# Token mixer of a two-layer block: groups of score products and of transposes split around halves of projections

## The reference, cut to what matters

```python
for i in range(DEPTH):                       # DEPTH = 2, 256 tokens, D = 1024
    h = rmsnorm(x, norm_mix[i])
    x = x + token_mixer(h, w_in[i], ...)     # the part that is changed
    x = x + peer(rmsnorm(x, norm_ffn[i]), ...)
return rmsnorm(x, norm_final)

def token_mixer(h, ...):                     # c = h @ w_in, split by columns
    o_ret = retention(q, k, v, g, norm)      # scores * decay, values, norm, gate
    o_moba = moba(q, k, v)                   # causal softmax attention, 4 heads
    o_ssm = mamba2(z, xbc, dt, ...)          # convolution, scores * exp(segment sums), norm
    o_nsa = nsa(q, cmp, slc, win, gate, ...) # compressed, selected and window attention
    return concatenate([o_ret, o_moba, o_ssm, o_nsa]) @ w_out
```

## Time and profile before

| what | value |
| --- | --- |
| runs | 1931.24, 1931.28, 1932.91 us; median 1931.28 |
| profiled execution | 1932.08 us |
| its span, first to last instruction | 1930.2 us |
| granted TensorE clock | 0.997 |
| PE busy | 1909.7 us, 99% of the span |
| DVE, POOL, ACT busy | 1289.6, 1245.1, 996.0 us |
| mixer of layer 0 | about 60 to 166 us of the span |
| mixer of layer 1 | about 1015 to 1122 us |

### The profile page before, as it was taken

The page is one execution under the profiler, slowest core; times in us unless marked ns, Lnnn a source line. Parts: engine busy times, 40 slices in busy tenths (PEclk is TensorE's granted clock), DMA queues, the critical chain, the costliest instruction groups (busy, mean ns, idle before and its releaser), DMA issues. The chain is left out here.

```text
span 1930.2 us, 38013 instructions
## 1 busy us (share of the span) xinstructions
PE 1909.7 (99%) x12350; PEld 1699.9 (88%) x12350; DVE 1289.6 (67%) x2922; ACT 996.0 (52%) x1581; POOL 1245.1 (65%) x626
## 2 busy tenths in 40 slices
PE   9999999999999999999999999999999999999998
PEld 9888888899999888888898888888999998888886
DVE  5656799789997444444466558996899964444444
ACT  5655444654444554455466544447544454455444
POOL 6447788877776555555574477888777765555553
PEclk9999999999999999999999999999999999999999
DMA  6525555554444566555545255555444455555553
GB/s 221 185 89 164 191 191 185 185 173 154 152 160 165 196 189 193 195 194 189 185 164 179 88 175 197 185 187 185 162 161 154 159 170 193 195 191 193 194 196 130
DMA packets 93240, 338.40 MB, mean 175 GB/s; under 512 B 10352, under 2 KB 10736, under 8 KB 93168
## 3 DMA queue, kind: packets, MB, share of 16 engines
q1 hardware_dynamic: 93168, 337.54, 52.0%
HBM read 336.45 MB, written 1.05 MB: 175 GB/s over the span
## 5 line engine op out<-in xcount | busy, mean ns | idle before, releaser
L491 POOL TENSOR_TENSOR WL<-ring,WH 128x1024 fp32r<-128x1024 f32 x360 | 867.7, 2413 | 342.6 <-ACT WH L1405 174.6
L1405 ACT CAST WH<-ring 128x1024 fp32r<-128x1024 f32 x512 | 538.4, 1052 | 695.5 <-PE PS L1099 329.4
L520 POOL TENSOR_TENSOR HX<-G,HX 128x256 fp32r<-128x256 f32 x256 | 371.4, 1451 | 320.9 <-ACT HX L1514 320.9
L2140 DVE TENSOR_TENSOR WL<-ring,WH 128x1024 fp32r<-128x1024 f32 x248 | 303.9, 1225 | 370.9 <-ACT WH L1405 370.9
L1099 PE MATMUL PS<-WH,HX 128*128 128x512 f32 x2048 | 506.2, 389 | 0.0
L1099 PEld LDWEIGHTS PS<-WH,HX 128*128 128x128 f32 x2048 | 384.3, 188 | 79.8
L989 PE MATMUL PS<-HX,WH 128*128 128x512 f32 x1248 | 313.2, 393 | 0.0
L1099 PE MATMUL PS<-WL,HX 128*128 128x512 f32 x1024 | 274.0, 389 | 0.0
L989 PEld LDWEIGHTS PS<-HX,WH 128*128 128x128 f32 x1248 | 224.5, 189 | 40.3
L1031 PE MATMUL PS<-HX,WH 128*128 128x256 f32 x1024 | 255.9, 288 | 0.0
L1032 PE MATMUL PS<-HX,WH 128*128 128x256 f32 x1024 | 250.6, 283 | 0.0
(11 more groups left out here) (262 smaller groups left out, 2084.3 us busy)
## 6 DMA issues: line engine op xcount, KB each, us to landing
ring<-stream SPq DMA_DIRECT2D x636, 512.0 KB, 3.3
X<-x_t SPq DMA_DIRECT2D x4, 256.0 KB, 4.1
out_t<-X SPq DMA_DIRECT2D x2, 512.0 KB, 2.7
CN<-consts SPq DMA_DIRECT2D x1, 851.0 KB, 9.4
WF<-last SPq DMA_DIRECT2D x1, 512.0 KB, 9.7
PR<-params SPq DMA_DIRECT2D x2, 239.0 KB, 4.4
CN<-consts SPq DMA_DIRECT2D x1, 64.0 KB, 3.2
```

What stands on the lines that cost most here:

```text
L491: nc.gpsimd.tensor_tensor(WL[:, b, :], ring[:, slot, :], WH[:, b, :].bitcast(F32), ALU.subtract).then_inc(done, 1)
L520: nc.gpsimd.tensor_tensor(GL[:, s, :], G[:, tile, :], GH[:, s, :].bitcast(F32), ALU.subtract).then_inc(L.gl_ready, 1)
L1405: nc.scalar.copy(WH[:, b, :], ring[:, slot, :]).then_inc(L.hi_ready, 1)
L2140: V.tensor_tensor(WL[:, s % 2, :], ring[:, (U0 + s) % SLOTS, :], WH[:, s % 2, :].bitcast(F32), ALU.subtract).then_inc(L.vlo_ready, 1)
```

## The change

It moves instructions and adds none. (1) The turns of the window branch go in two pairs of heads around unit 13's second half; those of the selected branch around `compress(6)` and unit 14's second half, which now comes before the state-space values. `compress(7)` and the turns of MoBA's queries and keys follow those values at once. (2) MoBA's and the retention's scores go two and two around units 15's and 17's second halves. (3) MoBA's last three turns of probabilities alternate with the retention's values, MoBA's own values wait for the fourth head's copy only before the fourth head, and the fourth `m_turn` comes four halves of the output projection later, behind the first half of piece 2. (4) On ACT the copies and casts follow that order, and the second square root moves behind the third `taken_m`. (5) On DVE `lower_m(0)` goes behind the square of the retention's output, and the second norm's sums behind `lower_m(1)`.

```diff
-                    def turn_group(buf, g):
-                        for h in range(NH):
+                    def turn_group(buf, g, heads=range(NH)):
+                        for h in heads:
...
                     compress(4)
-                    turn_group(SC4[0], 0)
+                    turn_group(SC4[0], 0, (0, 1))
                     project(13, (1,))
+                    turn_group(SC4[0], 0, (2, 3))
                     compress(5)
                     project(14, (0,))
-                    turn_group(SC4[1], 1)
+                    turn_group(SC4[1], 1, (0, 1))
                     compress(6)
+                    project(14, (1,))
+                    turn_group(SC4[1], 1, (2, 3))
                     pe.wait_ge(L.seg_ready, 4)
                     pe.wait_ge(L.ps_ready, 2)
                     values(lambda h: SEG[:, h, :], lambda h: [XDT[:, t, h * HD:(h + 1) * HD] for t in range(TT)])
-                    project(14, (1,))
                     compress(7)
+                    pe.wait_ge(L.roped, 3)
+                    turn(columns(MOBA_Q))
+                    turn(columns(MOBA_K))
                     pe.wait_ge(L.tr_evac, 8)
                     pe.wait_ge(L.pv_evac, 1)
                     values(lambda h: PT[0][:, h, :], y_values(V_WIN, 0))
...
-                    pe.wait_ge(L.roped, 3)
-                    turn(columns(MOBA_Q))
-                    turn(columns(MOBA_K))
                     project(15, (0,))
...
-                    for h in range(NH):
+                    for h in (0, 1):
                         scores(half(TQ_MOBA + h // 2, h), half(TK_MOBA + h // 2, h), True)
                     project(15, (1,))
+                    for h in (2, 3):
+                        scores(half(TQ_MOBA + h // 2, h), half(TK_MOBA + h // 2, h), True)
...
-                    turn_group(SC4[0], 2)
+                    turn_group(SC4[0], 2, (0, 1))
+                    pe.wait_ge(L.sc_evac, 18)
+                    values(lambda h: SC4[1][:, h, :], y_values(RET_V, HD), 7, (0, 1))
+                    turn_group(SC4[0], 2, (2,))
+                    values(lambda h: SC4[1][:, h, :], y_values(RET_V, HD), 7, (2, 3))
+                    turn_group(SC4[0], 2, (3,))
...
                     out_piece(1, 0)
+                    out_piece(1, 1)
+                    pe.wait_ge(L.hl_ready, DC + 3)
+                    out_piece(2, 0)
                     m_turn(3, L.m_ready, 3)
-                    out_piece(1, 1)
...
                     exps(1, SC4[1], (0, 1))
-                    probabilities(PT[0])
+                    probabilities(PT[0], (0, 1))
                     upper(2 * PROJ.index(14))
                     exps(1, SC4[1], (2, 3))
+                    probabilities(PT[0], (2, 3))
+                    upper(2 * PROJ.index(14) + 1)
                     take(13, next_too=False)
                     act.wait_ge(L.seg_ready, 4)
                     nc.scalar.activation(SEG[:, :, :], SEG[:, :, :], ACT.Exp).then_inc(seg_exp, 1)
-                    probabilities(PT[1])
-                    upper(2 * PROJ.index(14) + 1)
+                    probabilities(PT[1], (0, 1))
                     upper(2 * PROJ.index(15))
                     take(14, next_too=False)
+                    probabilities(PT[1], (2, 3))
+                    upper(2 * PROJ.index(15) + 1)
...
                     rough_root(rvar, rroot, L.g_var, g_rs, 1)
-                    rough_root(gvar, groot[:, 0:4], L.g_var, g_rs, 2)
                     upper(first_out + 2)
                     taken_m(1)
                     upper(first_out + 3)
                     taken_m(2)
-                    upper(first_out + 4)
+                    rough_root(gvar, groot[:, 0:4], L.g_var, g_rs, 2)
+                    for q in (4, 5, 6):
+                        upper(first_out + q)
                     taken_m(3)
```

More of the change, by code:

```diff
@@ L675, in half, with values @@
                         return T[(h % 2) * HD:(h % 2) * HD + HD, block, :]
-                    def values(weights, v, b=6):
-                        for h in range(NH):
+                    def values(weights, v, b=6, heads=range(NH)):
+                        for h in heads:
                             w, vh = weights(h), v(h)
@@ L684, in values @@
                             mm = nc.tensor.matmul(o, w[:, 2 * P:3 * P], vh[1], start=False, stop=True)
-                        mm.then_inc(L.pv_done, 1)
+                        if NH - 1 in heads:
+                            mm.then_inc(L.pv_done, 1)
                     def y_values(c, step):
                         return lambda h: [Y[:, t, c + h * step:c + h * step + HD] for t in range(TT)]
-                    def turn_group(buf, g):
-                        for h in range(NH):
+                    def turn_group(buf, g, heads=range(NH)):
+                        for h in heads:
                             pe.wait_ge(L.exp_done, 8 * g + 2 * h + 2)
@@ L859, in _ @@
                     pe.wait_ge(L.tr_evac, 16)
-                    for h in range(NH):
+                    for h in (0, 1):
                         scores(half(TK_RET + h // 2, h), half(TQ_RET + h // 2, h), False)
                     project(17, (1,))
+                    for h in (2, 3):
+                        scores(half(TK_RET + h // 2, h), half(TQ_RET + h // 2, h), False)
                     pe.wait_ge(L.tr_evac, 17)
@@ L928, in _ @@
                     m_turn(0, L.m_ready, 1)
-                    pe.wait_ge(L.sc_evac, 18)
-                    values(lambda h: SC4[1][:, h, :], y_values(RET_V, HD), 7)
+                    pe.wait_ge(L.pv_evac, 4)
+                    values(lambda h: PT[0][:, h, :], y_values(MOBA_V, HD), heads=(0, 1, 2))
                     pe.wait_ge(L.tr_evac, 21)
-                    pe.wait_ge(L.pv_evac, 4)
-                    values(lambda h: PT[0][:, h, :], y_values(MOBA_V, HD))
+                    values(lambda h: PT[0][:, h, :], y_values(MOBA_V, HD), heads=(3,))
                     pe.wait_ge(L.evac, len(PROJ) - N_XBC)
@@ L942, in _ @@
                     out_piece(1, 0)
+                    out_piece(1, 1)
+                    pe.wait_ge(L.hl_ready, DC + 3)
+                    out_piece(2, 0)
                     m_turn(3, L.m_ready, 3)
-                    out_piece(1, 1)
[L945 to L948, removed]
+                    out_piece(2, 1)
+                    pe.wait_ge(L.hl_ready, DC + 4)
+                    out_piece(3, 0)
+                    out_piece(3, 1)
                     pe.wait_ge(L.x_added, 3)
@@ L1235, in exps, with probabilities @@
                                                      accum_out=rsum[g][:, k:k + 1]).then_inc(L.exp_done, 1)
-                    def probabilities(buf):
-                        for h in range(NH):
+                    def probabilities(buf, heads=range(NH)):
+                        for h in heads:
                             taken(buf[:, h, :], 384).then_inc(L.tr_evac, 1)
@@ L1325, in _ @@
                     nc.scalar.activation(SEG[:, :, :], SEG[:, :, :], ACT.Exp).then_inc(seg_exp, 1)
-                    probabilities(PT[1])
-                    upper(2 * PROJ.index(14) + 1)
+                    probabilities(PT[1], (0, 1))
                     upper(2 * PROJ.index(15))
                     take(14, next_too=False)
+                    probabilities(PT[1], (2, 3))
+                    upper(2 * PROJ.index(15) + 1)
                     act.wait_ge(L.piece_done, slot_of_w1(7) + 1)
                     nc.scalar.copy(HID[:, :, :], bank[7].rearrange("p (s n) -> p s n", s=2)).then_inc(L.hid_ready, 1)
-                    upper(2 * PROJ.index(15) + 1)
                     act.wait_ge(padded, 2 * layer + 2)
@@ L1374, in _ @@
                     taken_m(2)
-                    upper(first_out + 4)
+                    rough_root(gvar, groot[:, 0:4], L.g_var, g_rs, 2)
+                    for q in (4, 5, 6):
+                        upper(first_out + q)
                     taken_m(3)
-                    for q in range(5, 2 * N_OUT + 1):
+                    for q in range(7, 2 * N_OUT + 1):
                         upper(first_out + q)
@@ L1885, in _ @@
                     dve.wait_ge(silu_done, 2 * layer + 2)
-                    lower_m(0)
                     ra, rb = TB[:, 1024:1536], TB[:, 1536:2048]
@@ L1893, in _ @@
                     step(V.tensor_tensor(rb, ra, ra, ALU.mult))
+                    lower_m(0)
                     step(V.tensor_reduce(rvar, rb.rearrange("p (k n) -> p k n", n=HD), AX.X, ALU.add))
                     V.tensor_scalar(rvar, rvar, 1.0 / HD, EPS, ALU.mult, ALU.add).then_inc(L.g_var, 1)
[L1897 to L1900, removed]
                     nsa_factor(2, None)
@@ L1912, in _ @@
                     lower_m(1)
+                    step(V.tensor_tensor(ya, ya, TB[:, 512:1024].rearrange("p (t n) -> p t n", t=TT), ALU.mult))
+                    step(V.tensor_tensor(yb.rearrange("p (t n) -> p t n", t=TT), ya, ya, ALU.mult))
```

(4 more changed lines are left out.)

## The result

The changed kernel takes 1940.85 us (1940.65 to 1941.97, five runs) against 1931.37 before (1931.24 to 1932.91): ratio 1.0047, 95% interval 1.0034 to 1.0060. It is 9.5 us slower. The profiled execution's span went from 1930.2 to 1939.0 us.

A forecast was written before the change was run, and what follows sets the result against it. PE, busy 99% of the span, was taken to bound the kernel. Per layer, 5.4 us removed against 3.7 and 0.4 added gave -1.3, -2.6 in all: 1928.7 us, 0.13% faster, range 1923.5 to 1933.5.

The forecast's parts named there:

- the price of the wait: At the first window value, PE waiting for bank 6 was priced at its length alone, 3.7 us a layer.
- -5.4 + 3.7 + 0.4 a layer: Mixer sum: stalls removed, window-value wait added, second square root's loss added; -1.3 us a layer.
- both its causes: Before bank 6's release: SEG's chain slips behind unit 14's cast, and POOL's subtractions hold two rotation operations; 3.7 us wait.
- the forecast 2.95 (0.5 and 2.45): DVE after POOL's pair: held rotation ends 0.5 us later, then the remaining operations through bank 6's evacuation take 2.45.
- the "slower" rival: Output projection: sums held by two subtractions delay root and casts; total +2.2 to +5.8 us, 1933.5 to 1937.1; chance 0.12.
- forecast 5.4: All PE stalls removed in one layer's mixer: 0.6 + 0.6 + 1.15 + 1.2 + 1.35 + 0.5 us.
- the forecast 1.35: From MoBA's last turns to the first `m_turn`: retention's values between the turns remove 1.35 us a layer.
- 0.67 for 0.5: At the second `m_turn`: DVE reaches its source earlier, removing its 0.47 us idle; with the drain 0.5 a layer.
- The 1.2 for the turns: Window and selected branches: groups of six turns no longer stall on ACT's copies, 0.6 us each per layer.
- The second square root: Ahead of output-projection casts on ACT, waiting for DVE's sums: 0.4 us lost a layer, between 0.1 and 0.6.
- The hold: In DVE's rotation: an operation with both operands in SBUF waits out POOL's subtraction; two operations held after the change.
- The 0.55 us: A DVE operation with both operands in SBUF, falling under POOL's subtraction, ends 0.55 us after it.

The follow-up runs named there:

- e2: Changed kernel with 34 unused transposes added on PE ahead of the window values, filling the wait: 1931.29 us, ratio 1.0001.
- e1: Changed kernel with DVE's add that evacuates bank 6 moved ahead of the rotation: 1925.36 us, ratio 0.9965.
- e4: Kernel before with eight more DVE additions ahead of the one that evacuates bank 6, putting a wait in: 1951.09 us, ratio 1.0098.
- e5: Changed kernel with part 1 and its share of part 4 undone, the rest as changed: 1923.84 us, ratio 0.9963.
- e9: e5 with the window and selected branches' turns halved in place, unit 14's second half left behind the state-space values: 1925.25 us.
- e6: e5 with ACT's second square root behind the cast of half 4 instead of ahead of it: 1927.27 us, ratio 0.9977.
- e7: e1 with ACT's second square root behind the cast of half 4 instead of ahead of it: 1925.99 us, ratio 0.9972.
- e3: Changed kernel with the add that evacuates bank 6 behind the rotation's third operation, two operations earlier: 1936.57 us, ratio 1.0024.
- e8: Changed kernel with ACT's cast of unit 15's second half behind the copy of bank 7, so POOL's second subtraction starts later: 1933.62 us, ratio 1.0008.
- e10: The kernel of e5 timed once more, unchanged, as the base for e9: 1924.35 us.

## Why the prediction was wrong

**The step that failed is the price of the wait.** The prediction took -5.4 + 3.7 + 0.4 a layer, that is, a wait of PE at its own length. Its place, its length, both its causes and its repetition in layer 1 were right, the length with some luck: with the first mark's 1.1 us taken off, POOL's pair was forecast to end at 98.9 and ended at 99.63, and from there to the end of L1851 it took 2.46 us for the forecast 2.95 (0.5 and 2.45). But a wait of 3.8 us lowered the clock behind it, and that cost another 4.7 us a layer, more than the wait. It stood in no term, no rival and no chance: the "slower" rival was the root, a mechanism that the runs did not show at that size. e2 removes the clock's share alone: its layer 0 is 109.57 - 104.92 = 4.65 us shorter. e1 removes wait and clock, 8.72, of which the wait is 4.04. e4 adds both to a kernel without the change, and the clock's share is 5.8 there. In layer 0 the parts add up: -5.3 removed (4.67 + 0.65 from e1, see below; forecast 5.4), +4.04 wait, +0.65 root, +4.66 clock make 4.05, as in the ledger.

The trace of before could have warned. PE idles 1.76 us before 10.47 us, and the clock falls to 0.50 at about 11.9 and stays there until about 15.3: 0.83 in the stretch from 10 to 20 us. A forecast that gives PE, busy at 99%, a new idle of several microseconds needs a term for the clock.

**What was removed, term by term.** Six turns take 0.64 us (81.23 to 81.87), two heads' scores 0.86, both in MoBA's and in the retention's group, as forecast. From the last branch's turns to the output projection it is 6.93 instead of 8.44 us, 1.5 won for the forecast 1.35, and the first half with its `m_turn` takes 3.22 instead of 3.89, 0.67 for 0.5. In e1's layer 0, where no new wait for bank 6 is, the whole comes to 4.67 after the loss to POOL; 5.4 - 0.4 = 5.0 was forecast, and 0.25 of what is missing is the root (below). The 1.2 for the turns was won only where something covered SEG's product, in e1's layer 0 (100.85 against e5's 102.05); in e1's layer 1 the late piece took it away (below), and in e9 it was nothing. I had counted stalls at a place and not asked what PE would then reach too early.

**The second square root.** The wait for POOL is 0.30 us, and the half with it takes 161.52 - 158.15 = 3.37 instead of 2.72 (before, 156.31 to 159.03): 0.65, where I took 0.4 and gave 0.6 as the bound. The sign and the cause were right (e6, e7); that moving the root behind the cast would help, as e6 and e7 expected, was wrong.

**A late piece, not forecast.** In layer 1 PE waits 0.7 us for unit 14's second half and 0.3 for its remainder. ACT began that cast the moment the piece landed, at 1050.12, 5.3 us after its slot came free at 1044.82; in layer 0 it was 3.6. The same wait appears in e1, e3, e7 and e8, all with part 1, and not in e2; it goes with a layer 1 that is 1.4 us longer than layer 0 in e1, of which the two waits are 1.0. Part 1 asks for this piece with less time to spare; why it lands late in one layer only stays open.

**The hold** of a VectorE operation under POOL's subtraction is now shown by an edit (e8), not only read from rows. The 0.55 us that the prediction read at its end is right for 128x512 and too long for 128x256, where it is 0.28.

**Which kernel is best.** e5 (1923.8 and 1924.4), e1 (1925.4) and e9 (1925.3) all beat the kernel before by 6 to 8 us and the changed one by more than 15, and their intervals overlap. e5 is the simplest: the change without its first part. Nothing here combines e5 with the release of bank 6 put first, which would take away what e6's layer 0 shows; it stays untried.

## What to carry to other kernels

When a reordering makes PE wait anew, price the wait twice: its length, and what the following work costs at half the clock. Here that was 3.8 and 4.7 us. Before splitting a group to fill a stall, follow PE to the next value that it will reach earlier, and check that this value is ready. And where a buffer's release stands in an engine's list behind long operations that don't need it, put the release first: three moved lines were worth 15.5 us in the changed kernel. In the kernel before, where the add ended 1.6 us ahead of its use, no wait stood there to be won.

## What the runs showed of the hardware

- Among the waits of PE that were read, the clock fell to 0.50 behind those of 4.28 and 4.25 (e4), 3.93 and 3.79 (after), 2.48 and 2.36 (e3), 1.76 (before, at 10.47), 1.73 (e10, at 10.27) and 1.66 us (e8). It stayed at 1.00 behind those of 2.22 (e3, at 10.92), 1.88 (e8), 1.86 (after, at 10.83), 1.71 (e5, at 10.73), 1.26 (e6), 1.24 and 1.15 us (e9). Between 1.66 and 2.22 us both happened.
- The fall could come while PE still waited (e4) or up to 1.9 us after it had begun again (e8). The price of one, in the same stretch of work, was 3.1 us (e8), 4.5 to 4.7 (e3, after) and 5.8 (e4).
- Thirty-four transposes whose result nobody reads kept the clock up, and saved 9.6 us in the program (e2).
- A VectorE operation with both operands in SBUF that fell under POOL's subtraction ended 0.54 to 0.56 us after it when it had 128x512 elements (103.57 after 103.02 in e8, 99.19 after 98.65 in e6) and 0.28 us after it with 128x256 (99.91 after 99.63 in the changed kernel, 99.03 after 98.75 in e8). The eight in e4 that read PSUM took 5.77 us together, 0.72 each, although a subtraction ran beside the last of them from 102.24 us.
